# Expanding eight distance-bias rows onto 128 rows each: from one SBUF partition, or by way of a DRAM copy

## The chip, the cores and the metric

One NeuronCore of a Trainium2 chip runs the whole program; the other seven are idle. The metric is the device time of one execution in microseconds (us). Of the kernel before, three timed executions were taken: 3765.06, 3767.77 and 3768.7 us, median 3767.77. A further execution ran under the hardware profiler.

## The reference

The program is one mixture block followed by two hybrid layers, on 512 tokens of width 1024, all in float32. The part that matters here is the first of its steps. The tokens are projected by `w_in`, and the projections feed four branches. Two of the branches are attentions with four heads each, and both add a bias to the scores that depends only on the head and on the distance between query and key:

```python
bias = jnp.transpose(bias_tab[_t5_bucket(rdist * dilation)], (2, 0, 1))        # branch a
s = jnp.einsum('bnqhd,bnkhd->bnhqk', qb, kb).astype(jnp.float32) * dh ** -0.5 + bias
...
bias = jnp.moveaxis(bias_tab[_t5_bucket(dist)], -1, 2)                          # branch b
logits = jnp.where((dist >= 0)[:, :, None, :], logits + bias, -jnp.inf)
```

So for each of the 8 heads there is one row of 1024 numbers, indexed by distance, and the attention wants it as a matrix in which every query has that row moved on by one place.

## The kernel before, in words

The program is a chain of stages. A stage is a block in which each engine has its own program; at the end of a stage all engines meet at a barrier. The stages that concern us are the first few.

**`project`** is the first stage. It multiplies the tokens with `w_in`. The weights come as a stream of chunks of 1 MB (128 partitions x 2048 float32), and each chunk holds 16 blocks of 128x128. A chunk passes through three hands:

- SP loads it from DRAM into one of two buffers `w_raw` (`Stream.load`, L118). The load of chunk c waits until chunk c-2 has been split, since it takes its buffer.
- POOL splits it into a rounded part `w_hi` (L129) and a remainder `w_lo` (L132) (`Stream.divide`). These have two buffers too: the split of chunk c waits for the load of c and for PE to have begun chunk c-1.
- PE multiplies: three matmuls a block against the two halves of the tokens (`product`, L156 to L158), 8 blocks to a tile of 128 output columns. There are 21 tiles, j = 0 to 20, each copied out of PSUM by DVE into `pj` (L307). Two wide outputs follow, `av` and `cv`, of 16 blocks each (`product_tm`, L164 to L166), copied out by DVE at L313. So the stage uses 200 blocks, chunks 0 to 12, with half of chunk 12 left for later.

POOL also splits chunk 13 ahead, for a later stage, once PE has begun chunk 12, and SP then issues the load of chunk 15. Only then can the stage end.

**`distance_bias`** runs beside it. After tile j = 10 PE multiplies a table of buckets with the bias table (L679), and DVE copies the result, 8 rows of 1024 float32, into `bias_rows`, on partitions 0 to 7 (L685). ACT then issues eight DMAs (L673), one for each head: each reads one row, which is 4 KB in one partition, 128 times, and writes it to 128 successive rows of the DRAM tensor `distance_bias`, 512 KB. ACT waits for all of them before it leaves the stage (`bias_stored`).

**`mixers_ab`** comes after. Several small stages lie ahead of `attention`, and there SP loads for each head the `strips` from `distance_bias` (L570) with a row step of 1023 elements, so that every partition gets the row moved by one place. That is why the row is stored 128 times.

The order of the work is thus set by four queues: SP's loads of weights, ACT's DMAs for the bias, POOL's splits in the order of the chunks, and PE's own order. SP's and ACT's DMAs run on the same 16 DMA engines.

Of the kernel before, what the change touches and what calls it, by code (L numbers as in the profile page):

```python
# [16 lines left out]
F32 = mybir.dt.float32  # L17
# [165 lines left out]
@contextmanager  # L183
def memory(k, **shapes):

    with ExitStack() as ctx:
        out = []
        for name, shape in shapes.items():
            dt = F32
            if shape[0] in ("r", "i"):  # L190
                dt, shape = (F32R if shape[0] == "r" else mybir.dt.int32), shape[1:]
            k.tensors += 1
            out.append(ctx.enter_context(k.nc.sbuf_tensor(f"{name}_{k.tensors}", [128, *shape], dt)))
        yield out[0] if len(out) == 1 else out
# [9 lines left out]
def split_start(k):  # L204

    names = ("zeroed", "consts_in", "x_in", "rounded_x", "split_x")

    def scalar(act, zeroed, consts_in, x_in, rounded_x, split_x):
        for t in range(KT):
            act.dma_start(k.res[:, t, :], k.dram["xT"][:, t, :]).then_inc(x_in, 16)  # L210
        act.dma_start(k.consts[:, :], k.dram["consts"]).then_inc(consts_in, 16)
        act.dma_start(k.par1[:, :], k.dram["params1"]).then_inc(consts_in, 16)
        act.dma_start(k.mats1[:, :], k.dram["mats1"]).then_inc(consts_in, 16)
        act.wait_ge(consts_in, 48)

    def gpsimd(pool, zeroed, *_):
        pool.wait_ge(zeroed, 1)

    def tensor(pe, t, zeroed, consts_in, x_in, rounded_x, split_x):
        pe.wait_ge(split_x, t + 1)  # L220

    def vector(dve, zeroed, consts_in, x_in, rounded_x, split_x):
        dve.memset(k.ws.zero[:, :], 0.0).then_inc(zeroed, 1)
        dve.memset(k.eps[:, 0:1], 1e-5).then_inc(zeroed, 1)
        dve.memset(k.eps[:, 1:2], 1e-6).then_inc(zeroed, 1)
        dve.memset(k.eps[:, 2:3], 64e-5).then_inc(zeroed, 1)
        dve.memset(k.eps[:, 3:4], 1.0).then_inc(zeroed, 1)
        dve.memset(k.eps[:, 4:5], 1e-5 / ALPHA ** 2).then_inc(zeroed, 1)
        for t in range(KT):
            if t == 0:  # L230
                dve.wait_ge(x_in, 16 * KT)
            dve.tensor_copy(k.xh[:, t, :], k.res[:, t, :]).then_inc(rounded_x, 1)
            dve.wait_ge(rounded_x, t + 1)
            dve.tensor_tensor(k.xl[:, t, :], k.res[:, t, :], k.xh[:, t, :].bitcast(F32), ALU.subtract).then_inc(
                split_x, 1)
    return names, dict(scalar=scalar, gpsimd=gpsimd, tensor=tensor, vector=vector)
# [422 lines left out]
def distance_bias(k, bias_dram, rows, tab, out):  # L659

    names = ("rows_in", "bias_ready", "bias_copied", "bias_stored")

    def loads(sp, rows_in, *_):
        sp.dma_start(rows[0:34, :], k.dram["dist_rows"]).then_inc(rows_in, 16)
        sp.dma_start(tab[0:34, :], k.dram["rpb"]).then_inc(rows_in, 16)

    def scalar(act, rows_in, bias_ready, bias_copied, bias_stored):
        act.wait_ge(bias_copied, 2)  # L670
        for h in range(8):
            row = out[h:h + 1, :].rearrange("p (a x) -> p a x", a=1).to_broadcast([1, 128, 1024])
            act.dma_start(bias_dram[h:h + 1, :, :], row).then_inc(bias_stored, 16)  # L673
        act.wait_ge(bias_stored, 128)

    def tensor(pe, rows_in, bias_ready, bias_copied, bias_stored):
        pe.wait_ge(rows_in, 32)
        for j in range(2):
            pe.matmul(k.bank[2 + j][0:8, :], tab[0:34, :], rows[0:34, 512 * j:512 * j + 512], start=True,  # L679
                      stop=True).then_inc(bias_ready, 1)  # L680

    def vector(dve, rows_in, bias_ready, bias_copied, bias_stored):
        for j in range(2):
            dve.wait_ge(bias_ready, j + 1)
            dve.tensor_copy(out[0:8, 512 * j:512 * j + 512], k.bank[2 + j][0:8, :]).then_inc(bias_copied, 1)  # L685
    return names, dict(loads=loads, scalar=scalar, tensor=tensor, vector=vector)
# [1439 lines left out]
def store_out(k, c0):  # L2126
    ws = k.ws
    end = c0 + LAYERS * LAYER_CHUNKS
    with stage(k, "stored") as (block, stored):
        @block.sync  # L2130
        def _(sp):
            sp.dma_start(k.dram["outT"], k.res[:, :, :]).then_inc(stored, 16)
            sp.wait_ge(stored, 16)
            for c in (end + 1, end + 2):
                sp.wait_ge(ws.loaded[c % SLOTS], 16 * (c // SLOTS + 1))


def build(nc, dram):
    with ExitStack() as ctx:
        k = Kernel(nc, dram)  # L2140
        k.bank = [ctx.enter_context(nc.psum_tensor(f"bank{b}", [128, 512], F32)) for b in range(8)]
        k.ws = Stream(nc, ctx, dram["weights"])
        k.ws.limit = FIRST_CHUNKS
        k.xh, k.xl, k.res, k.consts, k.par1, k.par2, k.mats1, k.mats2, k.eps = ctx.enter_context(memory(
            k, xh=("r", KT, SEQ), xl=("r", KT, SEQ), res=(KT, SEQ), consts=(CONSTS,), par1=(P1_COLS,),
            par2=(P2_COLS,), mats1=(548,), mats2=(256,), eps=(5,)))
        bias_dram = nc.dram_tensor("distance_bias", (8, 128, 1024), F32, kind="Internal").ap()
        k.rows_dram = nc.dram_tensor("token_rows", (SEQ, D), F32, kind="Internal").ap()
        k.picked_dram = nc.dram_tensor("picked_rows", (2 * SEQ, D), F32, kind="Internal").ap()
        grid_dram = nc.dram_tensor("grid_bias", (60, 4096), F32, kind="Internal").ap()  # L2150
        with memory(k, yb=(KT, SEQ)) as k.yb:
            with memory(k, pj=(T1_TILES, SEQ), av=(4, 256), cv=(4, 256)) as (pj, av, cv):
                with memory(k, rows=(1024,), tab=(8,), bias_rows=(1024,)) as (rows, tab, bias_rows):
                    project(k, T1_TILES, pj, [(av, 256), (cv, 256)], first=split_start(k),
                            aside=distance_bias(k, bias_dram, rows, tab, bias_rows))
                mixers_ab(k, pj, av, bias_dram)
                mixer_c(k, pj, cv)
                mixer_d(k, pj, av, cv)
            merge(k, ALPHA, k.dram["xT"])
        par = lambda n, j: k.par1[:, P1[n] + j:P1[n] + j + 1]  # L2160

        moe(k, lambda t: par("ln_g", t), lambda t: par("ln_b", t), lambda t: par("ln_g", 8 + t),
            lambda t: par("ln_b", 8 + t))
        c0 = k.ws.blocks // 16
        with nc.Fori(0, LAYERS) as i:
            k.ws.turn = i * LAYER_CHUNKS
            layer(k, i, grid_dram)
            assert k.ws.blocks == 16 * (c0 + LAYER_CHUNKS)
        store_out(k, c0)
# [231 lines left out]
```

## Time and profile before

| | us |
|---|---|
| median of three timed executions | 3767.77 |
| the three executions | 3765.06 to 3768.7 |
| the profiled execution, its own time | 3771.5 |
| its span, first to last instruction | 3769.7 |
| mean granted TensorE clock, share of full | 0.871 |
| PE busy | 3068.9 (81% of the span) |
| DVE busy | 1734.7 (46%) |
| POOL busy | 1521.4 (40%) |
| ACT busy | 645.7 (17%) |

The profiled execution is 3.7 us above the median and 1.8 us above its own span. A profile of this kind gives, for each engine, the busy time, and for each idle stretch what ended it. Read the shares of the whole span with care: the program has stages with quite different limits, so the question is always which wait ends last in the stage that is changed.

### The profile page before, as it was taken

What the parts mean: (1) busy time and instruction counts of PE and PEld (TensorE: products, weight loads), DVE (VectorE), ACT (ScalarE), POOL (GpSimd) and SP (SyncE); (2) the same over time, 40 slices, a digit from 0 to 9 for tenths busy, and PEclk for the clock granted to TensorE, in tenths of its full rate; (3) what the DMA queues carried; (4) which work ended last, traced back from release to release, by engine and by line L of the source; (5) the groups of instructions that cost most, each with busy time, mean ns of one, the idle gap of its engine ahead of it and who ended that gap; (6) DMA issues with size and microseconds to landing.
All of it is one profiled execution on the core that took longest, in us unless ns stands there. A gap on an engine that the chain in (4) does not pass through costs nothing. (4 is left out here: it accounts for less than half of the span.)

```text
span 3769.7 us, 33430 instructions
## 1 busy us (share of the span) xinstructions
PE 3068.9 (81%) x12858; PEld 2268.9 (60%) x12858; DVE 1734.7 (46%) x2065; ACT 645.7 (17%) x1005; POOL 1521.4 (40%) x430
## 2 busy tenths in 40 slices
PE   6633935889978999678578998999794689989999
PEld 5432524768756666447236876887573258858877
DVE  2007445544336666432365335881213464337840
ACT  0001220010024555321231001000103130010000
POOL 5230000047611111135005765776462027747766
PEclk9865557989988999778679998999896799989999
DMA  3970000012226888412011221222221202212223
GB/s 133 61 74 15 25 1 0 1 67 100 79 113 255 319 312 321 187 63 78 27 27 58 100 90 65 92 90 89 87 89 49 27 23 91 100 67 86 94 90 112
DMA packets 77110, 353.79 MB, mean 94 GB/s; under 512 B 30900, under 2 KB 31284, under 8 KB 38358
## 3 DMA queue, kind: packets, MB, share of 16 engines
q1 hardware_dynamic: 62824, 333.03, 24.7%
q10 hardware_dynamic: 2886, 10.10, 4.1%
q0 software_dynamic: 11232, 8.43, 0.7%
q8 instruction: 105, 1.72, 0.2%
q14 instruction: 63, 0.52, 0.0%
HBM read 353.19 MB, written 30.80 MB: 102 GB/s over the span
## 5 line engine op out<-in xcount | busy, mean ns | idle before, releaser
L129 POOL TENSOR_TENSOR w_hi<-w_raw,w_zero 128x2048 fp32r<-128x2048 f32 x174 | 627.7, 3607 | 1798.4 <-PE bank L156 1641.9
L156 PE MATMUL bank<-xh,w_hi 128*128 128x512 f32 x1864 | 754.2, 405 | 146.5 <-POOL w_lo L132 53.1
L132 POOL TENSOR_TENSOR w_lo<-w_raw,w_hi 128x2048 fp32r<-128x2048 f32 x174 | 812.8, 4671 | 13.6
L157 PE MATMUL bank<-xl,w_hi 128*128 128x512 f32 x1864 | 749.6, 402 | 0.0
L158 PE MATMUL bank<-xh,w_lo 128*128 128x512 f32 x1864 | 747.9, 401 | 0.0
L156 PEld LDWEIGHTS bank<-xh,w_hi 128*128 128x128 f32 x1864 | 357.1, 192 | 253.9 <-issue 98.3
L158 PEld LDWEIGHTS bank<-xh,w_lo 128*128 128x128 f32 x1864 | 357.8, 192 | 88.4
L157 PEld LDWEIGHTS bank<-xl,w_hi 128*128 128x128 f32 x1864 | 358.4, 192 | 85.1
L499 DVE TENSOR_TENSOR part<-sig,bank 128x512 f32<-128x512 f32 x96 | 66.1, 689 | 382.1 <-PE bank L158 381.7
L2119 DVE TENSOR_TENSOR fl<-work,fh 128x512 fp32r<-128x512 f32 x44 | 211.2, 4801 | 1.5
L536 DVE SCALAR_TENSOR_TENSOR res<-res,bank 128x512 f32<-128x512 f32 x40 | 27.5, 688 | 375.7 <-PE bank L158 375.7
L1502 POOL DMA_INDIRECT picked_rows<-work,ids x39 | 39.2, 1006 | 332.4 <-DVE work L1787 264.9
L307 DVE COPY pj<-bank 128x512 f32<-128x512 f32 x49 | 33.9, 692 | 293.7 <-PE bank L158 293.7
L484 ACT ACTIVATE sig<-bank 128x512 f32<-128x512 f32 x96 | 57.6, 600 | 637.6 <-PE bank L158 637.6
L503 DVE TENSOR_TENSOR part<-part 128x512 f32<-128x512 f32 x72 | 148.1, 2058 | 2.4
L156 PE MATMUL bank<-fh,w_hi 128*128 128x512 f32 x352 | 140.8, 400 | 7.8 <-PEq L180 7.8
L2118 DVE CAST fh<-work 128x512 fp32r<-128x512 f32 x44 | 144.4, 3282 | 1.5
L157 PE MATMUL bank<-fl,w_hi 128*128 128x512 f32 x352 | 140.1, 398 | 0.0
L158 PE MATMUL bank<-fh,w_lo 128*128 128x512 f32 x352 | 140.0, 398 | 0.0
L579 PE MATMUL bank<-pj 64*128 64x512 f32 (+3 forms) x128 | 87.3, 784 | 55.7 <-PEq L180 55.7
L1774 DVE TENSOR_TENSOR xl<-raw,xh 128x2048 fp32r<-128x2048 f32 x38 | 87.0, 2290 | 54.5 <-ACT xh L1616 54.5
L1774 DVE TENSOR_TENSOR w_lo<-w_raw,w_hi 128x2048 fp32r<-128x2048 f32 x40 | 91.5, 2290 | 40.3 <-ACT w_hi L1616 40.2
(497 smaller groups left out, 4820.0 us busy)
## 6 DMA issues: line engine op xcount, KB each, us to landing
w_raw<-weights SPq DMA_DIRECT2D x216, 1024.0 KB, 4.8
raw<-weights SPq DMA_DIRECT2D x51, 1024.0 KB, 8.9
res<-weights SPq DMA_DIRECT2D x26, 1024.0 KB, 6.2
distance_bias<-bias_rows ACTq DMA_DIRECT2D x8, 512.0 KB, 72.9
na_bias<-grid_bias SPq DMA_DIRECT2D x16, 240.0 KB, 7.0
strips<-distance_bias SPq DMA_DIRECT2D x8, 448.0 KB, 3.1
raw<-picked_rows SPq DMA_DIRECT2D x6, 512.0 KB, 6.5
tabs<-tables SPq DMA_DIRECT2D x2, 1408.0 KB, 6.3
```

The costliest lines, as they stand in the source:

```text
L129: pool.tensor_tensor(self.hi[:, s, :], self.raw[:, s, :], self.zero[:, 0:1].to_broadcast([128, CHUNK]), ALU.add).then_inc(self.rounded, 1)
L132: pool.tensor_tensor(self.lo[:, s, :], self.raw[:, s, :], self.hi[:, s, :].bitcast(F32), ALU.subtract).then_inc(self.split, 1)
L156: self.released(pe.matmul(out, hi, moving[0], start=start, stop=False))
L157: pe.matmul(out, hi, moving[1], start=False, stop=False)
L158: return pe.matmul(out, lo, moving[0], start=False, stop=stop)
L484: act.activation(sig[:, u % 2, :], k.bank[2 * (u % 2)][:, :], ACT.Sigmoid).then_inc(sigmoid_ready, 1)
L499: dve.tensor_tensor(part[:, 0 if n == 0 else 1, :], sig[:, u % 2, :], k.bank[2 * (u % 2) + 1][:, :], ALU.mult).then_inc(banks_free, 1)
L503: step(dve.tensor_tensor(part[:, 0, :], part[:, 0, :], part[:, 1, :], ALU.add))
L579: pe.matmul(score_bank(i)[:, 0:u["n"]], u["q"], u["keys"], start=True, stop=True).then_inc(scores_ready, 1)
L1774: dve.tensor_tensor(g_lo[c % 4], g_raw[c % 4], g_hi[c % 4].bitcast(F32), ALU.subtract).then_inc(g_split, 1)
L2118: step(dve.tensor_copy(fh[:, j, :], mid[:, 0, :]))
L2119: step(dve.tensor_tensor(fl[:, j, :], mid[:, 0, :], fh[:, j, :].bitcast(F32), ALU.subtract))
```

## The change

The eight rows are first stored to a new DRAM tensor `distance_bias_once` (8 x 1024), by one DMA of 32 KB. ACT waits for it. Then the same eight DMAs are issued, each reading its row 128 times, but from that DRAM tensor and no longer from an SBUF partition. The destination and everything that reads it stay.

```diff
     def scalar(act, rows_in, bias_ready, bias_copied, bias_stored):
         act.wait_ge(bias_copied, 2)
+        act.dma_start(k.bias_once, out[0:8, :]).then_inc(bias_stored, 16)
+        act.wait_ge(bias_stored, 16)
         for h in range(8):
-            row = out[h:h + 1, :].rearrange("p (a x) -> p a x", a=1).to_broadcast([1, 128, 1024])
+            row = k.bias_once[h:h + 1, :].rearrange("p (a x) -> p a x", a=1).to_broadcast([1, 128, 1024])
             act.dma_start(bias_dram[h:h + 1, :, :], row).then_inc(bias_stored, 16)
-        act.wait_ge(bias_stored, 128)
+        act.wait_ge(bias_stored, 16 + 128)
...
+        k.bias_once = nc.dram_tensor("distance_bias_once", (8, 1024), F32, kind="Internal").ap()
         bias_dram = nc.dram_tensor("distance_bias", (8, 128, 1024), F32, kind="Internal").ap()
```

On ACT's queue, from the start of the program into the stage after `project`, the kernel before has:

```order
L211 DMA consts<-consts 128x2984
L212 DMA par_5<-params 128x57
L213 DMA mats_7<-mats 128x548
L673 DMA distance_bias<-bias_rows 128x1x1024 [waits bias_copied,consts_in]
L673 DMA distance_bias<-bias_rows 128x1x1024 x7
L176 UNCONDITIONAL_BRANCH [waits bias_stored]
```

and the changed kernel has there (its lines are two further on from here):

```order
L211 DMA consts<-consts 128x2984
L212 DMA par_5<-params 128x57
L213 DMA mats_7<-mats 128x548
L671 DMA distance_bias_once<-bias_rows 8x1024 [waits bias_copied,consts_in]
L675 DMA distance_bias<-distance_bias_once 128x1x1024 [waits bias_stored]
L675 DMA distance_bias<-distance_bias_once 128x1x1024 x7
L176 UNCONDITIONAL_BRANCH [waits bias_stored]
```

One DMA and one wait are new, the source of eight DMAs is another, and no other engine's instructions differ in kind, number or order.

## Rows read from the trace of the kernel before

**Rows 1.** The page: its span, and two rows of 40 slices of 94 us each.
```profile
span 3769.7 us, 33430 instructions
...
PEclk9865557989988999778679998999896799989999
DMA  3970000012226888412011221222221202212223
```

**Rows 2.** Busy time by stretch: stretch, its length, engines, granted clock, DMA share, GB/s.
```profile
40.00:97.00 57.00, 57.00 (x241) 44.39 (x240) 8.22 (x12) 0.00 (x0) 40.46 (x10) 1.00 0.21 74
97.00:251.70 154.70, 79.66 (x368) 65.90 (x367) 8.38 (x15) 0.00 (x0) 41.13 (x11) 0.76 0.96 60
251.70:273.00 21.30, 9.71 (x65) 9.29 (x63) 1.42 (x4) 0.00 (x0) 16.27 (x4) 0.76 0.31 113
```

**Rows 3.** The bias DMAs by tile: issue ns min/median/max, first and last start; landing.
```profile
L673 ACTq DMA_DIRECT2D distance_bias<-bias_rows x8: 584/12046/17019, 97.1 to 159.7; - x8
...
DMA to landing us min/median/max: 22.1/72.9/92.0
```

**Rows 4.** Waits from 97 to 275 us: engine, line, waited for: total, times, longest.
```profile
POOL w_hi L129 <- DMA w_raw<-weights: 110.8, 5, 34.1
DVE pj L307 <- PE bank L158: 109.1, 10, 35.4
...
PE bank L156 <- POOL w_lo L132: 53.1, 3, 28.6
```

**Rows 5.** The DMA queues from 97 to 251.7 us: packets, MB, share of 16 engines' time.
```profile
q10 hardware_dynamic: 1152, 4.19, 88.3%
q1 hardware_dynamic: 685, 5.04, 7.7%
```

**Rows 6.** The weight queue from 257 to 267 us, with one load of 1 MB alone.
```profile
q1 hardware_dynamic: 144, 1.05, 28.1%
```

**Rows 7.** POOL's splits in order of time: start, length, operation [idle before <- releaser].
```profile
89.30 3.60 POOL L129 TENSOR_TENSOR w_hi<-w_raw,w_zero 128x2048 fp32r<-128x2048 f32 x1 [2.91 <-PE bank L156]
...
102.52 3.60 POOL L129 TENSOR_TENSOR w_hi<-w_raw,w_zero 128x2048 fp32r<-128x2048 f32 x1 [4.96 <-PE bank L156]
...
123.80 3.60 POOL L129 TENSOR_TENSOR w_hi<-w_raw,w_zero 128x2048 fp32r<-128x2048 f32 x1 [12.99 <-DMA w_raw<-weights]
...
263.21 3.60 POOL L129 TENSOR_TENSOR w_hi<-w_raw,w_zero 128x2048 fp32r<-128x2048 f32 x1 [0.78 <-PE bank L164]
266.89 4.58 POOL L132 TENSOR_TENSOR w_lo<-w_raw,w_hi 128x2048 fp32r<-128x2048 f32 x1
```

**Rows 8.** DVE's copies of finished tiles in `project`, in order of time.
```profile
94.56 0.69 DVE L307 COPY pj<-bank 128x512 f32<-128x512 f32 x1 [4.91 <-PE bank L158]
...
102.17 0.69 DVE L307 COPY pj<-bank 128x512 f32<-128x512 f32 x1 [5.12 <-PE bank L158]
107.77 0.69 DVE L307 COPY pj<-bank 128x512 f32<-128x512 f32 x1 [4.91 <-PE bank L158]
...
270.25 1.42 DVE L313 COPY cv<-bank 128x256 f32<-128x256 f32 x4 [22.57 <-PE bank L166]
```

**Rows 9.** The first instruction of the stage after `project`, on ACT.
```profile
273.27 1.28 ACT L709 ACT_TABLE_LOAD   x1 [273.27 <-PEq L180]
```

**Rows 10.** DVE's copies in the same function in layer 1, no bias DMAs beside it.
```profile
1731.69 0.69 DVE L307 COPY pj<-bank 128x512 f32<-128x512 f32 x1 [4.90 <-PE bank L158]
1743.05 1.42 DVE L313 COPY rv<-bank 128x256 f32<-128x256 f32 x4 [10.66 <-PE bank L166]
1756.25 1.42 DVE L313 COPY nv<-bank 128x256 f32<-128x256 f32 x4 [11.79 <-PE bank L166]
```

**Rows 11.** SP's loads of chunks 8 and 9: first start, and time to the second's end.
```profile
97.58 13.58 SPq L118 DMA_DIRECT2D w_raw<-weights  x2
```

**Rows 12.** DMA issues of the whole page: KB each, median us from issue to landing.
```profile
w_raw<-weights SPq DMA_DIRECT2D x216, 1024.0 KB, 4.8
...
strips<-distance_bias SPq DMA_DIRECT2D x8, 448.0 KB, 3.1
...
token_rows<-xtm SPq DMA_DIRECT2D x4, 512.0 KB, 2.6
```

## The prediction

> **What bounds the kernel now.** I read the page's 40 slices first. In slices 1 and 2, about 94 to 283 us, the DMA engines are 9 and 7 tenths busy while TensorE's granted clock falls from 9 tenths to 8 and 6, and nowhere else do busy DMA engines stand over a falling clock like this [rows 1]. Busy time by stretch says the same in numbers: from 40 to 97 us PE is busy all 57.0 us, at clock 1.00 with a DMA share of 0.21; from 97 to 251.7 us PE is busy 79.7 of 154.7 us at clock 0.76, with a DMA share of 0.96 that moves only 60 GB/s [rows 2]. The reader is to see full DMA engines that move little.
>
> The bias DMAs by tile date the stretch. The first is issued at 97.1 us, the last at 159.7, and the longest takes 92.0 us to land [rows 3], so the last lands by 251.7. The waits name the victim: POOL stands still for 110.8 us, five times, for loads of weights, PE in turn for POOL, and DVE 109.1 us for PE [rows 4]. POOL's own order shows the turn: the split at 89.30 us came after the usual 2.91 us for PE; the one at 123.80 came after 12.99 us, for a DMA [rows 7]. The chain through this stage is therefore weight load, POOL, PE, and the load is slow because ACT's queue holds the engines: in the stretch its packets took 88.3% of the 16 engines' time for 4.19 MB, and the weights' packets 7.7% for 5.04 MB [rows 5].
>
> **The prices of a packet.** 4.19 MB in rows of 4 KB are 1,024 packets of data (the other 128 of 1,152 are the eight DMAs' 16 completions each). 154.7 us x 16 engines x 0.883 / 1,024 = 2.13 us for 4 KB, in total 4.19 MB / 154.7 us = 27 GB/s. A load of weights alone has 128 data packets of 8 KB; 10 us x 16 x 0.281 / 128 = 0.35 us [rows 6]. The copy of half the size takes six times as long.
>
> Which side of the copy is slow, the reading of one partition or the writing to DRAM? The writes of `token_rows` to DRAM, from 128 partitions, land in 2.6 us for 512 KB, and the `strips`, 448 KB read from DRAM, in 3.1 us [rows 12]. A copy of 512 KB at 27 GB/s takes 19 us. So writing to DRAM is not slow in itself and the one 4 KB source remains. The Trainium skill says why it might be (SBUF — State Buffer, Door 1: The DMA port swizzle): DMA bandwidth depends on how many of 16 ports the partitions reach, and 16 ports make 435 GB/s, so one partition has 27. The measured 27 GB/s agrees with that.
>
> **The change, part by part.**
> *Removed:* eight DMAs with a single partition as source.
> *Added, the store:* 32 KB from 8 partitions to DRAM, and a wait on ACT. Lower bound nothing, upper the 4.8 us of a 1 MB load [rows 12]; I take 3 us, nearest to the 2.6 us of the DRAM write. Behind ACT's wait only the eight copies are queued, and nobody waits for these before the stage's end, so on the path it costs nothing. Without that cover it would cost its 3 us.
> *Added, the copies:* no row shows DRAM to DRAM. Lower bound for a packet: 4 KB at the rate of the loads, half of 0.35, 0.17 us; 64 packets on each engine make 11 us. Upper bound: read and write one after the other and no DMA overlapping the next, (3.1 x 512/448 + 2.6) = 6.1 us for each of eight, 49 us, or 0.76 us a packet. I take the packet as 8 KB moved, 0.35 us, so 22 us, since successive DMAs of a queue overlap. The copies run from about 101 us to 123, at most to 150, and the stage still needs until 180, as follows.
>
> *The stage without starvation.* Tile j = 11 is copied at 102.17 and j = 12 at 107.77, 5.60 us apart [rows 8]; nine more tiles bring j = 20 to 102.17 + 9 x 5.60 = 152.57. For the two wide outputs the same function in layer 1 has 1743.05 - 1731.69 = 11.36 us and 1756.25 - 1743.05 = 13.20 us [rows 10], with loads of its own beside it. So `cv` is copied at 152.57 + 24.56 = 177.13 instead of 270.25, 93.1 us earlier. But POOL ends later than DVE here. It begins chunk 13 when PE begins chunk 12, which is half of `cv`, 5.7 us before 177.13, at 171.4; the split takes 8.26 us (263.21 to 271.47 [rows 7]), so it ends at 179.7, against 271.47: 91.8 us. SP's last load is issued behind it as before, and the next stage starts 1.8 us after the split as before, at 181.5 instead of 273.27 [rows 9]. **The gain is 91.8 us.**
>
> *Do the copies hide?* A load may take some time before PE feels it. Chunk 9 is requested at 97.58 + 13.58 - 0.33 = 110.8 us [rows 11] and, at 11.2 us a chunk (two tiles), wanted by POOL at 124.9; POOL idles 2.9 us a chunk [rows 7], which gives 17.0 us in all, against 4.8 alone [rows 12]. In the stretch, the weights got 5.04 MB / 8 KB = 615 data packets beside 1,024 copies, so 1.67 copies pass for each packet of weights [rows 5], and a load's 8 packets on each engine take 8 x (0.35 + 1.67p) us, p being a copy's packet. At p = 0.35 that is 7.5 us, under the 11.2 us of a chunk: hidden. At the upper bound, 0.76 us, it is 13.0 us, 1.8 us over the pace, for the four loads at most that meet the copies: 7.2 us late, of which the slack above the pace, 17.0 - 11.2 = 5.8, takes most. So 0 to 2 us are lost. I take nothing.
>
> *The rest of the program.* ACT has no other work until the stage ends, and `strips` are loaded from the same tensor only some stages later. Everything after moves up as a block. PE reaches the next stage from a busy stretch at clock 1.00, where it came from 0.76 before [rows 2]; this may give a few us and I count nothing, but let the range reach 8 us lower.
>
> **The sum.** Against the profiled execution: 3771.5 - 91.8 = 3679.7 us. It is 3.7 us above the median, so against the median 3676.0; with 1 us for copies not wholly hidden, **3677 us**.
>
> **Rivals.**
> *The copies are partly felt.* If 1,024 reads of one 4 KB row at a time slow DRAM too, but less than the partition did, say 50 GB/s: p = 1.3 us, a load takes 8 x (0.35 + 2.17) = 20.2 us, 9.0 us over the pace. Each engine's 64 copies and the 38 weight packets between them last 64 x 1.3 + 38 x 0.35 = 97 us and cover 4.8 loads: 43 us late, less 5.8 of slack, 37. That gives 3676 + 37 = 3713 us; at 36 GB/s (p = 1.8) the same working gives 3745. Against it: 16 engines read `strips` at 148 GB/s, landing included [rows 12]. For it: they read 128 different places, not one.
> *Nothing changes.* The bound of 2.13 us a packet lies in something that both forms share, the destination's 128 successive rows or ACT's queue; then the copies start 3 us later at the same rate: 3771 us, within the noise. The quick write of `token_rows` speaks against it.
> *Slower.* The one DRAM row is a narrower place than the one partition, in `project`, in the stretch after 97 us. It decides from p = 2.13 us upwards. At p = 2.6 the stretch of 154.7 us becomes 189, the weights starve in proportion, and with the 3 us of the store the time is 3768 + 34 + 3 = 3805 us. For it: each DRAM row is read by all 16 engines at once, and each packet now does two accesses to DRAM. Against it: the packets of one load, 0.35 us for 8 KB on 16 engines, are 375 GB/s [rows 6], fourteen times what the copies had.
> The Trainium skill has a rule that would bring this about (SBUF — State Buffer, A bandwidth-pool intuition that's wrong): DRAM is reached through 32 ports of about 22.5 GB/s each. By it a row behind one port would give 4.19 MB / 22.5 = 186 us, an estimate. Against that stands its page DMA: Bandwidth & Descriptors, Latency and other measured facts, where copies whose rows collide at a bad pitch still made 103 GB/s, an estimated 41 us here, which would hide. No row of this trace has many engines reading one place.
>
> **How the numbers follow.** Hidden, 3677 us: 0.77. Partly felt: 0.12. Nothing changes: 0.05. Slower: 0.06. A measurement tells 0.2%, 7.5 us, from no change. So faster 0.89, same 0.05, slower 0.06. Hidden runs from 3668 (warm clock) to about 3682; with the sizes unsure the range takes in half of the second case and ends at 3720.
>
> **What would show it.** In the changed profile: no wait of POOL for weights over 1 us after 102 us; the `pj` copies 5.60 us apart up to 152.6; `cv` copied at 177; the next stage at 181 to 182; the DRAM copies landing in under 10 us each once begun, ACT's queue empty before 150; packets of 0.2 to 0.8 us; clock 1.00 up to 177. It is wrong if a copy's packet takes over 1 us, if POOL waits for a load again, or if the stage ends with ACT waiting for the copies.

## The result, and the profile after

| | us |
|---|---|
| changed kernel, median of four executions | 3666.61 (3664.39 to 3668.12) |
| kernel before, median of four beside them | 3766.41 |
| ratio | 0.9734, 95% interval 0.9718 to 0.9751 |
| profiled execution of the changed kernel, span | 3664.1 |
| mean granted TensorE clock | 0.882 (0.871 before) |

The change gains 99.8 us between the medians. The forecast was 3677 us with a range from 3668 to 3720: the direction and the mechanism hold, but the time lies 10.4 us under the forecast and 1.4 us under the range. First the page, whose rows answer to [rows 1]. The starved slices 1 and 2 have become one full slice at clock 9, and the DMA row falls at once.

```profile
span 3664.1 us, 33431 instructions
...
PEclk9955569799979999696699999999896799989999
DMA  3300000122248887221202222222221212212223
```

Busy time by stretch of the changed kernel (stretch, its length, PE, PEld, DVE, ACT and POOL busy, granted clock, DMA share, GB/s), against [rows 2]:

```profile
40.00:97.00 57.00, 57.00 (x242) 44.36 (x241) 8.10 (x12) 0.00 (x0) 40.37 (x10) 1.00 0.21 74
97.00:180.00 83.00, 78.63 (x431) 67.31 (x429) 9.93 (x19) 0.00 (x0) 58.04 (x15) 1.00 0.42 140
```

PE is busy 78.6 of 83 us at full clock, where it was 79.7 of 154.7. The bias DMAs by tile, against [rows 3] (issue ns min/median/max, first and last start):

```profile
L675 ACTq DMA_DIRECT2D distance_bias<-distance_bias_once x8: 571/633/1202, 99.1 to 104.4; - x8
L671 ACTq DMA_DIRECT2D distance_bias_once<-bias_rows x1: 538/538/538, 97.3 to 97.3; - x1
```

Issuing a copy takes 0.6 us where it had taken 12.0 (a queue that is no longer full would explain it; no run tests that), and the store with its wait costs 99.1 - 97.3 = 1.8 us of ACT's free time. The DMA queues of the changed kernel from 99 to 116 us (packets, MB, share of 16 engines' time), against [rows 5]:

```profile
q10 hardware_dynamic: 1133, 4.14, 77.3%
q1 hardware_dynamic: 181, 1.35, 19.7%
```

Nearly all 4.19 MB of the copies go in 17 us, at 4.14 / 17 = 243 GB/s. A copy of 4 KB takes 17 x 16 x 0.773 / 1,011 = 0.21 us, against 2.13. The one load issued beside the copies lands in 9.6 us where a load alone takes 4.8, and that is still under the 11.2 us pace of the chunks. POOL, against [rows 7], no longer waits for a load at all; each wait is the usual one for PE:

```profile
102.64 3.60 POOL L129 TENSOR_TENSOR w_hi<-w_raw,w_zero 128x2048 fp32r<-128x2048 f32 x1 [4.96 <-PE bank L156]
...
113.84 3.60 POOL L129 TENSOR_TENSOR w_hi<-w_raw,w_zero 128x2048 fp32r<-128x2048 f32 x1 [2.91 <-PE bank L156]
...
171.73 3.60 POOL L129 TENSOR_TENSOR w_hi<-w_raw,w_zero 128x2048 fp32r<-128x2048 f32 x1 [4.90 <-PE bank L164]
175.41 4.54 POOL L132 TENSOR_TENSOR w_lo<-w_raw,w_hi 128x2048 fp32r<-128x2048 f32 x1
```

DVE's copies, against [rows 8], and the first instruction of the next stage on ACT, against [rows 9]:

```profile
152.69 0.69 DVE L307 COPY pj<-bank 128x512 f32<-128x512 f32 x1 [4.91 <-PE bank L158]
164.05 1.42 DVE L313 COPY av<-bank 128x256 f32<-128x256 f32 x4 [10.66 <-PE bank L166]
177.18 1.42 DVE L313 COPY cv<-bank 128x256 f32<-128x256 f32 x4 [11.72 <-PE bank L166]
```
```profile
181.75 1.28 ACT L711 ACT_TABLE_LOAD   x1 [181.75 <-PEq L180]
```

The forecast had 152.57, 177.13 and 181.5. The first stage gives 273.27 - 181.75 = 91.5 us. But the two spans differ by 3769.7 - 3664.1 = 105.6 us, so another 14 us lie behind the stage, in code that is the same. The mixture of experts has 6.4 of them (456.2 against 449.9 us), and the other stretches differ by 1 to 4 us each, not all in the same direction. The experiments have these two questions: is it the single partition, and what are the 14 us?

In what follows, **the first stage** runs to the first ACT instruction after it, and **the rest** from there to the end of the span: 3496.4 us before, 3482.3 after.

### The profile page after: what moved, and what is told of

The parts are those of the page before. It is cut to its first block and busy times, and to the rows that moved or that the text cites. A ratio compares the mean times of both kernels' runs of the same rounds, so it can differ in the third digit from the quotient of the medians.

```text
span 3664.1 us, 33431 instructions
## 1 busy us (share of the span) xinstructions
PE 3048.2 (83%) x12858; PEld 2257.0 (62%) x12858; DVE 1734.7 (47%) x2065; ACT 646.1 (18%) x1005; POOL 1522.0 (42%) x430
## 5 line engine op out<-in xcount | busy, mean ns | idle before, releaser
L1776 DVE TENSOR_TENSOR w_lo<-w_raw,w_hi 128x2048 fp32r<-128x2048 f32 x40 | 91.5, 2289 | 39.3 <-ACT w_hi L1618 39.2
```

The costliest lines, as they stand in the source:

```text
L1776: dve.tensor_tensor(g_lo[c % 4], g_raw[c % 4], g_hi[c % 4].bitcast(F32), ALU.subtract).then_inc(g_split, 1)
```

## Experiments on the cause: which side of the copy was slow

**Keep the store, copy from SBUF again.** Against the changed kernel:

```diff
-            row = k.bias_once[h:h + 1, :].rearrange("p (a x) -> p a x", a=1).to_broadcast([1, 128, 1024])
+            row = out[h:h + 1, :].rearrange("p (a x) -> p a x", a=1).to_broadcast([1, 128, 1024])
```

> The new DRAM tensor, the store and its wait are kept, but the eight copies read the SBUF partitions again. Theory S (the one 4 KB partition as source limits the copies): the copies take about 155 us again, about 2 us later than before, POOL waits over 100 us for weights, and the time is 3767 to 3771 us. Rival on the part of the gain that lies behind the stage (99.8 us were gained, 91.5 of them in the first stage): if the other 8 us come from the new tensor, which moves the DRAM tensors allocated after it, this kernel has them too, and takes 3759 to 3763 us.

Measured: 3774.8 us median of ten executions, mean 3770.1, ratio of the means to before 1.0018 (0.9998 to 1.0039). POOL waits in this kernel from 97 to 295 us, against [rows 4]:

```profile
POOL w_hi L129 <- DMA w_raw<-weights: 115.2, 3, 56.5
```

The whole gain is gone, so it hangs on the source, and the extra store brings nothing by itself. The median is 4 us over what was expected and the mean is inside it, because the ten executions scatter more than those of any other kernel here: eight lie between 3766 and 3779 us, two at 3751 and 3753. The profiled one took 3776.5 us; its first stage ends at 288.4 us, 15 later than before, and three long waits have taken the place of five. No quick one was profiled, so why two of ten were quick stays open.

**Half the heads from each source.**

```diff
         for h in range(8):
-            row = k.bias_once[h:h + 1, :].rearrange("p (a x) -> p a x", a=1).to_broadcast([1, 128, 1024])
+            src = k.bias_once if h < 4 else out
+            row = src[h:h + 1, :].rearrange("p (a x) -> p a x", a=1).to_broadcast([1, 128, 1024])
```

> Heads 0 to 3 are copied from the DRAM rows, heads 4 to 7 from their SBUF partitions. Theory S: 2.1 MB at 27 GB/s keep the DMA engines for about 77 us instead of 155; the time is about halfway, 3705 to 3720 us, and POOL waits 45 to 60 us for weights. Rival Q (the limit lies in the number of copies in ACT's queue or in the destination, and the DRAM source only happens to be better placed): no clear half, or the four SBUF copies are quick with the queue half empty and the time stays within 5 us of 3667.

Measured: 3729.3 us, ratio 0.9908 (0.989 to 0.9927). The first stage ends at 239.1, 57.5 us after the changed kernel's: a dose does give a part of the effect, as the source theory wants, though less than half: 35 of 96 us of the gain stay. POOL's wait for weights, a single one of 60.5 us, is just over the expected 45 to 60, and the time is 9 us over its range. The reason is in how the wait falls. The queues from 113 to 148 us and then from 148 to 183:

```profile
q10 hardware_dynamic: 264, 0.95, 94.8%
```
```profile
q10 hardware_dynamic: 248, 0.88, 81.7%
q1 hardware_dynamic: 248, 1.86, 12.6%
```

In the first 35 us the weight queue has no row: with a load pending, not one of its packets went through while the slow copies moved 27 GB/s. Then it caught up. The 1.67 copies for each packet of weights in the prediction were only an average over the stretch; how the engines choose between the two queues is not shown.

**One DMA that reads eight partitions.** No DRAM hop; against the kernel before:

```diff
-        for h in range(8):
-            row = out[h:h + 1, :].rearrange("p (a x) -> p a x", a=1).to_broadcast([1, 128, 1024])
-            act.dma_start(bias_dram[h:h + 1, :, :], row).then_inc(bias_stored, 16)
-        act.wait_ge(bias_stored, 128)
+        row = out[0:8, :].rearrange("p (a x) -> p a x", a=1).to_broadcast([8, 128, 1024])
+        act.dma_start(bias_dram[:, :, :], row).then_inc(bias_stored, 16)
+        act.wait_ge(bias_stored, 16)
```

> No DRAM hop. One DMA of 4 MB for all heads, source the 8 rows on SBUF partitions 0 to 7, 128 times each, so that several partitions are read at once. Theory S with the limit in a port that four neighbouring partitions share (two ports here): about 54 GB/s, the copy takes 75 to 85 us, the weights are little or partly delayed, 3667 to 3700 us. If the limit is each partition's own: 8 times as fast as one, the copy takes 20 to 30 us, 3667 us. Rival Q: 155 us again and 3760 to 3770 us.

**The same DMA with the eight rows four partitions apart.** The source is `out[0:32:4, :]`; the bias table has 32 columns instead of 8, with each fourth in use, so that the matmul of L679 writes 32 rows.

> The same single DMA, but the 8 rows lie on partitions 0, 4, 8 to 28, by a bias table with 32 columns of which each fourth is used. Theory S with shared ports: eight ports, the copy takes 20 to 35 us, less than half of what partitions 0 to 7 need, and the time is 3664 to 3670 us. If the limit is each partition's own: the same as with partitions 0 to 7. Rival Q: 155 us again and 3760 to 3770 us.

Measured: 3687.0 us (ratio 0.9793, 0.9774 to 0.9813) for partitions 0 to 7, and 3666.8 us (ratio 0.9746, 0.9724 to 0.9768) for partitions 0, 4, 8 to 28. The queue of the copy from 99 to 119 us in the first and then in the second:

```profile
q10 hardware_dynamic: 247, 1.01, 42.0%
```
```profile
q10 hardware_dynamic: 710, 2.91, 35.3%
```

1.01 MB in 20 us are 50 GB/s and 2.91 MB are 145 GB/s. In the first kernel the rate goes on like this to 179 us and 0.26 MB are left after it; in the second all is done by 139. The 145 GB/s are an average over a stretch in which this copy had not begun (before 102 us) and one in which a load of weights ran beside it. Where the copy has the engines nearly to itself, the two kernels show this, the first from 104 to 112 us, the second from 103 to 113:

```profile
q10 hardware_dynamic: 97, 0.40, 47.4%
```
```profile
q10 hardware_dynamic: 509, 2.08, 50.6%
```

That is 50 GB/s against 208. Same number of DMAs, same size, same destination, same number of source rows; only their distance differs. So the limit of the near kernel is neither the destination nor the queue (rival Q would have had 3760 us or more), nor each partition's own, for then both kernels would be alike. It is shared by neighbours: one partition gives 27 GB/s, eight adjacent ones together only twice that.

The Trainium skill has just this (SBUF — State Buffer, Door 1: The DMA port swizzle): four neighbouring partitions sit on one port, so 0 to 7 reach two ports and 0, 4 to 28 reach eight. At 27 GB/s a port two ports would give 54, an estimate, and 50 were measured; eight would give 217, also an estimate, and 208 were measured while the copy ran nearly alone.

The two rows also show that either copy occupies only half of the 16 engines' time, 47% and 51%, where the old one had 97% of it in a like stretch (100 to 108 us). A packet of the far kernel takes 10 x 16 x 0.506 / 509 = 0.16 us, which is half of the 0.35 us of a weight packet of twice the size, so the far kernel may be held by its half of the engines and not by the eight ports; the runs do not part these.

The expectation for the near rows was 75 to 85 us for the copy; some 85 are measured (99 us to about 184). The weights are partly delayed, POOL waits 32.2 us for them, and the time is in the expected range. Against the kernel before, this one gains 77 us with its source still in SBUF, but two ways of reading changed together, several rows at once and one DMA that takes half of the engines, and no run says which share is whose.

## Experiments on the 14 us behind the stage

My first guess was that the rest's length hangs on the moment at which it starts. Idle activations on ACT were put between the first stage and the rest of the changed kernel:

```diff
+                idle(k, N)
                 mixers_ab(k, pj, av, bias_dram)
...
+def idle(k, n):
+    with stage(k, "idled") as (block, idled):
+        @block.scalar
+        def _(act):
+            for i in range(n):
+                act.activation(k.yb[:, 0, :], k.xh[:, 0, :].bitcast(F32), ACT.Square).then_inc(idled, 1)
+                act.wait_ge(idled, i + 1)
```

> The changed kernel with a stage of 14 dependent ACT activations put between the projection and the attention mixers, about 14 us of nothing for the other engines. Its length is read from the profile; what counts is the rest, from the stage after it to the end: 3482.4 us in the changed kernel's profile, 3496.4 in that of the kernel before. Theory P (the rest's length hangs on the moment at which it starts, through when the TensorE clock moves between its two levels): the rest differs from 3482 by several us, either way. Rival H (the rest is shorter because of the new tensor's place in DRAM, or because of what happened in the first stage, and not because of when it starts): 3482 within 2 us.

> The same with 50 activations, about 43 us. Theory P: a rest that differs from 3482 and from that of the run with 14, anywhere from 3478 to 3500. Rival H: 3482 within 2 us, and a time that is the changed kernel's 3666.6 plus the length of the idle stage.

> The same with 110 activations, about 92 us, so that the rest starts about where it did in the kernel before. Theory P: the rest is near 3490 to 3497, and the whole near that of the kernel before, 3762 to 3770 us. Rival H: the rest is 3482 and the whole is 3666.6 + 92 = 3759 us.

The changed kernel and the kernel before were also profiled again, unchanged:

> The changed kernel once more, with a second profile. Theory P: the rest behind the first stage is 3482 us within 3, since the program starts in the same way each time. If the length of the rest is chance from run to run, it may lie anywhere between 3478 and 3500 us. The time is 3664 to 3669 us either way.

> The kernel before, profiled again, to see how much its two parts vary: the first stage (273.3 us to the first instruction after it in the first profile) and the rest (3496.4 us). In five profiles with the changed kernel's loads the first stage ended at 181.0 to 181.8 us. Theory V (both parts vary by chance: the rest by when the TensorE clock moves, and the starved stage by how the two queues happen to share the engines): the first stage ends anywhere from 268 to 290 us and the rest is 3479 to 3496 us. Rival: the first stage ends at 273 within 1 us and the rest is 3494 to 3498, so that the change really shortens the rest.

> As before_p1, a further profile: theory V expects a first stage that differs from the other's by more than 1 us; the rival the same values again.

> As before_p1, a further profile: theory V expects the mean of the rests over the four profiles of the kernel before to be within 5 us of 3485, where those of the eight other kernels lie; the rival expects it above 3493.

> The changed kernel and the kernel before in five more rounds, to narrow the mean gain. The first stage ends at 273.3 to 274.2 us in four profiles of the kernel before and at 181.5 to 181.8 in two of the changed one, so it gives 92 us. Theory V (the rest is the same but for chance) expects a mean difference of 89 to 95 us in these rounds, and a first stage that ends at 181 to 182 us in the new profile. Rival (the rest is really a few us shorter) expects 95 to 100 us.

All profiles together; the last two kernels come up below. For the idle kernels the first stage is counted up to the first ACT instruction behind the idle stage:

| kernel | median us | first stage | rest |
|---|---|---|---|
| before | 3766.41 | 273.3 | 3496.4 |
| before, profile 2 | | 274.2 | 3480.3 |
| before, profile 3 | | 274.0 | 3496.9 |
| before, profile 4 | | 273.7 | 3493.4 |
| changed | 3666.61 | 181.75 | 3482.3 |
| changed, profile 2 | 3669.05 | 181.5 | 3492.8 |
| changed, profile 3 | 3665.10 | 181.4 | 3478.3 |
| idle, 14 | 3676.92 | 193.2 | 3491.7 |
| idle, 50 | 3697.32 | 216.6 | 3479.6 |
| idle, 110 | 3738.85 | 256.6 | 3479.5 |
| store, copies from SBUF | 3774.8 | 288.4 | 3486.3 |
| half the heads | 3729.31 | 239.1 | 3486.0 |
| one DMA, near | 3686.98 | 199.0 | 3485.8 |
| one DMA, far | 3666.77 | 181.8 | 3483.7 |
| store behind the old copies | 3764.72 | 274.0 | 3489.5 |
| changed, tensor behind the others | 3667.89 | 181.4 | 3478.3 |

In the two kernels that were profiled several times the first stage comes out the same within 1 us. The rest does not: 3480.3 to 3496.9 us in four executions of the kernel before, 3478.3 to 3492.8 in three of the changed one. That a later start lengthens it (theory P) falls: the idle stage of 110, which starts the rest at 257 us, has 3479.5, the opposite of the 3490 to 3497 it called for, and one and the same kernel moves by 14 to 17 us while its start moves by less than 1. The rival H, a rest of 3482 within 2 us, falls as well. (The idle activations took 0.66 us each, less than I had reckoned, so these stages are shorter than announced.)

Theory V of the later runs, that the rest varies from execution to execution, holds as far as that goes. Its numbers did not all come true. It let the first stage end anywhere from 268 to 290 us, and that is steady at 273.3 to 274.2. It wanted the four rests of the kernel before to have a mean within 5 us of 3485, its rival one above 3493: the mean is 3491.8. And it wanted 89 to 95 us between the means of the five further rounds, its rival 95 to 100: they are 96.1 us apart. Both misses lie on the side of a rest that is really somewhat shorter.

Where it varies can be seen in two stages of the layers, each with 76 PE instructions. The stretch between the loads of `tabs` and `share`, in both layers of the changed kernel's second profile and in both layers of its first (columns as in the stretches above):

```profile
1726.13:1794.46 68.33, 43.80 (x76) 14.49 (x76) 30.93 (x46) 15.55 (x19) 0.00 (x0) 0.67 0.06 21
2804.57:2873.13 68.56, 43.80 (x76) 14.48 (x76) 30.93 (x46) 15.54 (x19) 0.00 (x0) 0.67 0.06 21
```
```profile
1726.91:1792.23 65.32, 40.52 (x76) 13.78 (x76) 30.83 (x46) 15.55 (x19) 0.00 (x0) 0.71 0.06 22
2798.88:2864.24 65.36, 40.50 (x76) 13.79 (x76) 30.83 (x46) 15.54 (x19) 0.00 (x0) 0.71 0.07 22
```

and in the kernel before, its first profile:

```profile
1824.67:1893.22 68.55, 43.79 (x76) 14.48 (x76) 30.91 (x46) 15.55 (x19) 0.00 (x0) 0.67 0.06 21
2903.42:2966.22 62.80, 37.96 (x76) 12.93 (x76) 30.74 (x46) 15.44 (x19) 0.00 (x0) 0.77 0.06 23
```

The same instructions take 62.8, 65.3 or 68.5 us, at a mean granted clock of 0.77, 0.71 or 0.67, while DVE and ACT are busy equally long. The steps of about 3 us are the time by which PE works longer at the lower of its two levels. The mixture of experts varies too: from the store of `token_rows` to the loads of `picked_rows` the profiles of these two kernels have 446.0 to 456.2 us.

**Is any of it real?** With this scatter (standard deviation 5 us between executions) only means over many executions tell. One explanation could be tried: the new DRAM tensor moves the DRAM tensors allocated after it, which MoE and the layers read.

The first kernel is the kernel before with the tensor and, behind the eight old copies, the store:

```diff
         for h in range(8):
             row = out[h:h + 1, :].rearrange("p (a x) -> p a x", a=1).to_broadcast([1, 128, 1024])
             act.dma_start(bias_dram[h:h + 1, :, :], row).then_inc(bias_stored, 16)
-        act.wait_ge(bias_stored, 128)
+        act.dma_start(k.bias_once, out[0:8, :]).then_inc(bias_stored, 16)
+        act.wait_ge(bias_stored, 16 + 128)
...
+        k.bias_once = nc.dram_tensor("distance_bias_once", (8, 1024), F32, kind="Internal").ap()
         bias_dram = nc.dram_tensor("distance_bias", (8, 128, 1024), F32, kind="Internal").ap()
```

The second is the changed kernel with the tensor allocated behind all others:

```diff
-        k.bias_once = nc.dram_tensor("distance_bias_once", (8, 1024), F32, kind="Internal").ap()
         bias_dram = nc.dram_tensor("distance_bias", (8, 128, 1024), F32, kind="Internal").ap()
...
         grid_dram = nc.dram_tensor("grid_bias", (60, 4096), F32, kind="Internal").ap()
+        k.bias_once = nc.dram_tensor("distance_bias_once", (8, 1024), F32, kind="Internal").ap()
```

> The kernel before, with the new DRAM tensor allocated as in the changed kernel and the 32 KB store issued behind the eight old copies, so that it only adds the tensor. Theory T (the 4 us gained outside the first stage come from the DRAM tensors lying elsewhere): 3760 us, 4 us under the kernel before, with the first stage ending at 274 to 276. Theory V (chance, or something the tensor has no part in): 3764 to 3767 us, as the kernel before or up to 2 us more for the store.

> The changed kernel with the new tensor allocated behind all other DRAM tensors, which then lie where they did before. Theory T: 3672 us, 4 us over the changed kernel's 3668. Theory V: 3668 us within 3, and a first stage that ends at 181 to 182 us.

Measured: with the store behind the old copies 3764.7 us median of twelve (ratio 1.0006, 0.9996 to 1.0016), mean 3764.9, first stage 274.0; with the tensor behind the others 3667.9 us median of five, mean 3668.4, first stage 181.4. Theory T wanted 3760 and 3672 us. The first is 4.9 us off, some four times the standard error of twelve executions, so theory T falls; the second, 3.6 us off with five executions, would not be enough alone. Over all executions the kernel before has a mean of 3763.9 us (55 executions, 3752.3 to 3775.9) and the changed one 3668.1 us (13, 3661.0 to 3676.7): a gain of 95.8 us, with a standard error of 1.6 if all are taken as one sample; by sets of rounds it is 100.0, 94.4 and 96.1. The first stage gives 273.8 - 181.5 = 92.3 us of it. The remaining 3.5 us are about twice that error, and **whether they are real stays open**; of the 99.8 us of the first medians, at any rate, 4 are chance.

## Why the prediction was wrong, point by point

- **What bounds the stage**: right. Weight load, POOL, PE, held up by ACT's queue.
- **The source side is the slow one**: right, and now shown: with the store but the old source the gain is gone, and the distance of eight source rows alone moves the rate from 50 to 208 GB/s where the copy runs nearly alone.
- **A copy's packet, 0.35 us (0.17 to 0.76)**: 0.21 us, near the lower bound. I had counted a packet's reading and writing one after the other, and that was too dear; whether they overlap is not shown. The copies end at about 117 us, 6 earlier than I said; nobody waits for them either way.
- **The store, 3 us**: 1.8 us, hidden.
- **The stage without starvation, 91.8 us**: right; 91.5 us in the first pair of profiles, 92.3 as a mean. The tile pace, the two wide outputs taken from layer 1 and the split of chunk 13 as the last thing each came within 0.4 us. (The 5.7 us from the start of that split to `cv`'s copy came from no row; 177.18 - 171.73 = 5.45 were measured.)
- **The copies hide, 1 us of allowance**: they hide entirely, and the allowance was not needed. The load beside them landed in 9.6 us; the prediction's working gave 7.5 with its packet of 0.35 us and gives 5.6 with the measured 0.21, because it left out what a load takes even when alone (4.8 us, of which its packets explain 2.8).
- **The sum**: here it failed, at the step from one stage to the whole program. I took the median of three executions, 3767.77, as the kernel's time, and "everything after moves up as a block" as good to a few us. Over 55 executions the mean is 3763.9, and single ones lie 24 us apart. The 10.4 us between 3677 and 3666.6 divide so: 3.9 the base that was too high; 1.0 the allowance; 0.5 the first stage (92.3 against 91.8); 3.5 a shorter rest, whose cause stays open; 1.5 the four executions of the result, whose median lies under the mean of thirteen, 3668.1. No term of the first stage was off by more than 1 us on the path.
- **The range**: its low end, 3668, allowed 8 us for a warm clock, but nothing for the scatter of the rest, 18.6 us between the shortest and the longest in the profiles of all kernels. The mean of thirteen executions lies just on it, so whether four of them come out under it is luck. The warm clock itself brought nothing to see: the mixers behind the first stage (273.3 to 483.2 before, 181.8 to 391.7 after) take 209.9 and 209.95 us.
- **Rivals**: a DRAM row narrower than a partition is out, with 243 GB/s from eight rows that are read by one DMA after the other. By the Trainium skill's 22.5 GB/s for a DRAM port (SBUF — State Buffer, A bandwidth-pool intuition that's wrong) a row behind one port would have made it 186 us, an estimate; the copies took some 17, the measurement decides, and here a row is not held to one such port. "Nothing changes" and "partly felt" are out too, the latter because POOL waits for no load.
- **What a measurement can tell, 0.2%**: too sharp for a median of four, with single executions up to 0.3% off the mean.

## What to carry to other kernels

A broadcast DMA whose source is one SBUF partition filled all 16 DMA engines here and moved 27 GB/s; look for a full DMA row with few GB/s, and ask who else needs these engines. Spread the source over partitions (rows four partitions apart, in one DMA: 3666.8 us here) or pass by way of DRAM (3667 us): both cost nothing here, and neither is shown to be the better. And before a sum is set from a median of three, look at how far single stages with the same instructions lie apart; here the base was off by 3.9 us, more than all the terms of the change together.

## What the runs showed that I had not expected

- Slow copies do not share the engines fairly with another queue: with a load of weights pending, the weight queue had no packet for 35 us in the kernel with half the heads, where the average of the prediction would have let the load through. With the store ahead of the old copies, which starts them 2 us later, POOL waits three times in the profiled execution, 56.5 us at the longest, instead of five times and 34.1 at the longest; with the store behind them it waits as before.
- Eight rows of 4 KB in DRAM, each read 128 times and written elsewhere, moved at 243 GB/s beside a load of weights.
- One DMA for all eight rows used half of the 16 engines' time and was as good as the eight with all of them: 3666.8 us.
- A stage of 76 PE instructions with gaps between them came out at 62.8, 65.3 or 68.5 us, in steps that go with the granted clock (0.77, 0.71, 0.67), even within one execution.
